# Copying the turned attention probabilities for two heads in one operation instead of one head by each of two engines

## What is computed

```python
p = softmax(q @ k.T * scale + bias)     # each query against a window of its grid neighbours
o = p @ v                               # 8 heads of 64 columns
mix = head_rms_norm(concat[o, gmlp, fourier])
x = x + mix @ w_out
```

## Time and profile before

| | |
|---|---|
| median of 3 runs | 2064.92 us (2064.7 to 2065.62) |
| span of the profiled execution, first to last instruction | 2062.8 us |
| own time of the profiled execution | not given apart from its span; the span is 2.1 us below the median |
| PE busy | 2042.2 us, 99% |
| DVE busy | 1419.9 us, 69% |
| ACT busy | 825.1 us, 40% |
| POOL busy | 227.8 us, 11% |

### The profile page before, as it was taken

One profiled execution on the slowest core, in us unless ns is written; L12 is line 12 of the kernel. 1 busy time (PEld: TensorE's weight loads), 2 busy tenths in 40 slices (PEclk: granted clock), 3 DMA queues, 4 the chain that ended last, 5 costly groups with the idle time before them and its releaser, 6 DMA issues.

```text
span 2062.8 us, 27797 instructions
## 1 busy us (share of the span) xinstructions
PE 2042.2 (99%) x10316; PEld 1698.2 (82%) x10316; DVE 1419.9 (69%) x2320; ACT 825.1 (40%) x1466; POOL 227.8 (11%) x135
## 2 busy tenths in 40 slices
PE   8999999999999999999999999999999999999998
PEld 7888788888888888888898887888888888888887
DVE  6323773789877778787833338647988777778877
ACT  4221683452333333444612227634433333344443
POOL 1332034200000000000023301441000000000000
PEclk9999999999999999999999999999999999999999
DMA  5222443224333236633221314441243323383333
GB/s 183 72 92 62 144 134 123 72 77 169 130 111 107 98 112 255 195 97 97 76 86 62 102 41 144 144 153 48 85 172 129 114 93 111 109 310 114 97 98 123
DMA packets 111060, 244.40 MB, mean 118 GB/s; under 512 B 13648, under 2 KB 18640, under 8 KB 110672
## 3 DMA queue, kind: packets, MB, share of 16 engines
q1 hardware_dynamic: 97056, 214.32, 32.4%
q10 hardware_dynamic: 13872, 28.31, 3.7%
HBM read 191.73 MB, written 50.86 MB: 118 GB/s over the span
## 4 chain that ended last, share of the span: by engine, by line
PE 92%; DVE 5%; issue 1%; ACT 1%; DMA 0%; ACTq 0%; POOL 0%; DVEq 0%
PE bank L1872 28%; PE bank L1874 28%; PE bank L1873 28%; PE bank L2036 2%; PE bank L2055 2%; PE bank L2020 2%; DVE s_lo L1233 1%; DVE t_lo L1536 0%; PE bank L1966 0%; PE bank L2077 0%; PE bank L1995 0%; PE bank L2070 0%; ACT logits L950 0%; DVE hid_cu L1649 0%; ACT s_hi L797 0%
## 5 line engine op out<-in xcount | busy, mean ns | idle before, releaser
L1872 PE MATMUL bank<-t_hi,s_hi 128*128 128x512 f32 (+1 forms) x1336 | 516.9, 387 | 0.8 <-DVE hid_cu L1649 0.5
L1873 PE MATMUL bank<-t_lo,s_hi 128*128 128x512 f32 (+1 forms) x1336 | 516.3, 386 | 0.0
L1874 PE MATMUL bank<-t_hi,s_lo 128*128 128x512 f32 (+1 forms) x1336 | 516.3, 386 | 0.0
L1872 PEld LDWEIGHTS bank<-t_hi,s_hi 128*128 128x128 f32 x1336 | 250.9, 188 | 52.6 <-DVE hid_cu L1649 1.4
L1874 PEld LDWEIGHTS bank<-t_hi,s_lo 128*128 128x128 f32 x1336 | 250.9, 188 | 50.9
L1873 PEld LDWEIGHTS bank<-t_lo,s_hi 128*128 128x128 f32 x1336 | 250.9, 188 | 50.6
L675 POOL TENSOR_TENSOR w_lo<-w_raw,w_hi 128x1024 fp32r<-128x1024 f32 x65 | 161.1, 2492 | 928.9 <-ACT w_hi L761 787.4
L1872 PE MATMUL bank<-b_hi,s_hi 128*128 128x512 f32 x528 | 206.0, 390 | 0.2
L1874 PE MATMUL bank<-b_hi,s_lo 128*128 128x512 f32 x528 | 205.5, 389 | 0.0
L1873 PE MATMUL bank<-b_lo,s_hi 128*128 128x512 f32 x528 | 205.4, 389 | 0.0
L1872 PE MATMUL bank<-h_hi,w_hi 128*128 128x512 f32 x512 | 201.1, 393 | 0.0
(11 more groups left out here) (218 smaller groups left out, 3187.2 us busy)
## 6 DMA issues: line engine op xcount, KB each, us to landing
w_g<-in_wg SPq DMA_DIRECT2D x44, 512.0 KB, 3.5
w_u<-in_wu SPq DMA_DIRECT2D x44, 512.0 KB, 4.4
t_raw<-hidden_t SPq DMA_DIRECT2D x88, 256.0 KB, 2.6
bias<-in_bias SPq DMA_DIRECT2D x24, 768.0 KB, 5.8
w_raw<-in_win SPq DMA_DIRECT2D x34, 512.0 KB, 3.8
t_raw<-hidden_b SPq DMA_DIRECT2D x66, 256.0 KB, 2.6
hidden_b<-hid_g SPq DMA_DIRECT2D x60, 256.0 KB, 2.0
hidden_t<-hid_x SPq DMA_DIRECT2D x44, 256.0 KB, 2.0
```

The lines of the kernel that those rows point to most:

```text
L1872: nc.tensor.matmul(bank, lh, rh, start=start, stop=False)
L1873: nc.tensor.matmul(bank, lh, rl, start=False, stop=False)
L1874: return nc.tensor.matmul(bank, ll, rh, start=False, stop=stop)
```

## The change

Banks 2 and 3 become one tensor of two banks, `TURNED`. One operation now copies both heads of a pair, 128 x 768 elements, out of it: DVE does so for even pairs, ACT for odd pairs. Each copy waits for both heads of its pair to be turned. PE turns a pair only when the copy of the whole pair before it is done, and `values(i)` waits for one engine's counter instead of two. The DVE copies of heads 4m-2 and the ACT copies of heads 4m+1 vanish from the program; the others stay at their places and become pair copies. PE's instructions stay the same and in the same order.

```diff
-        B = [ctx.enter_context(nc.psum_tensor(f"bank{i}", [P, HALF], F32)) for i in range(8)]
+        B = [ctx.enter_context(nc.psum_tensor(f"bank{i}", [P, HALF], F32)) for i in range(2)]
+        TURNED = ctx.enter_context(nc.psum_tensor("turned", [P, 2, HALF], F32))
+        B += [TURNED[:, 0, :], TURNED[:, 1, :]]
+        B += [ctx.enter_context(nc.psum_tensor(f"bank{i}", [P, HALF], F32)) for i in range(4, 8)]
...
-                def turned_odd(t):
-                    act.wait_ge(pt_full, l * 64 + t + 1)
-                    if t >= 4:
-                        act.wait_ge(pv_done, l * 64 + t - 3)
-                    nc.scalar.activation(PT[:, t % 4, :], B[3][:, 0:NKEY], ACT.Copy).then_inc(pt_act, 1)
+                def turned_odd(i):
+                    act.wait_ge(pt_full, l * 64 + 2 * i + 2)
+                    if i >= 2:
+                        act.wait_ge(pv_done, l * 64 + 2 * i - 2)
+                    nc.scalar.activation(PT[:, 2:4, :], TURNED[:, :, 0:NKEY], ACT.Copy).then_inc(pt_act, 1)
...
                 for i in range(SINGLE):
                     if i:
                         probs(2 * i)
-                        turned_odd(2 * i - 1)
+                        if i % 2 == 0:
+                            turned_odd(i - 1)
                         probs(2 * i + 1)
...
                     probs(4 * m)
-                    turned_odd(4 * m - 1)
+                    turned_odd(2 * m - 1)
                     probs(4 * m + 1)
...
-                    turned_odd(4 * m + 1)
                 tile_raw(5)
-                turned_odd(63)
+                turned_odd(31)
...
-                def turned_even(t):
-                    dve.wait_ge(pt_full, l * 64 + t + 1)
-                    if t >= 4:
-                        dve.wait_ge(pv_done, l * 64 + t - 3)
-                    nc.vector.tensor_copy(PT[:, t % 4, :], B[2][:, 0:NKEY]).then_inc(pt_dve, 1)
+                def turned_even(i):
+                    dve.wait_ge(pt_full, l * 64 + 2 * i + 2)
+                    if i >= 2:
+                        dve.wait_ge(pv_done, l * 64 + 2 * i - 2)
+                    nc.vector.tensor_copy(PT[:, 0:2, :], TURNED[:, :, 0:NKEY]).then_inc(pt_dve, 1)
...
-                    if i:
-                        turned_even(2 * i - 2)
+                    if i % 2:
+                        turned_even(i - 1)
...
                     logits(4 * m)
                     logits(4 * m + 1)
-                    turned_even(4 * m - 2)
                     if m % 2:
                         head_norms((m - 5) // 2)
                     logits(4 * m + 2)
                     logits(4 * m + 3)
                     if m % 2 == 0:
                         head_sums((m - 4) // 2)
-                    turned_even(4 * m)
-                turned_even(62)
+                    turned_even(2 * m)
...
                     if t < 2:
                         pe.wait_ge(k_raw, l * 8 + 3 + t)
-                    else:
-                        pe.wait_ge(pt_act if t % 2 else pt_dve, l * 32 + t // 2)
+                    elif t % 2 == 0:
+                        pe.wait_ge(pt_dve if t % 4 else pt_act, l * 16 + (t + 2) // 4)
...
-                    pe.wait_ge(pt_dve, l * 32 + i + 1)
-                    pe.wait_ge(pt_act, l * 32 + i + 1)
+                    pe.wait_ge(pt_act if i % 2 else pt_dve, l * 16 + i // 2 + 1)
...
-                        pe.wait_ge(pt_act if b == 3 else pt_dve, l * 32 + 32)
+                        pe.wait_ge(pt_act, l * 16 + 16)
```

## The result

The changed kernel is slower: 2076.14 us against 2065.14 us in medians of four runs each, +11.0 us; the ratio is 1.0052 with a 95% interval of 1.0036 to 1.0068. One of the four runs of the changed kernel took 3445.01 us at a granted clock of 0.557 (one later run of the kernel before took 2932.92 us at 0.654) and is in that median but not in the ratio; the other three took 2075.21, 2075.70 and 2076.58 us. The prediction was 2077 us in a range of 2070 to 2082.

The account below looks back on a forecast made before the run. PE was taken to bound the kernel. Per layer 1.0 + 0.55 + 5 x 0.87 + 0.3 = 6.2 us, 12.4 for both, took the span from 2062.8 to 2075.2; with the median 2.1 above, 2077 us, range 2070 to 2082.

Parts of the forecast that it names:

- What bounds it: Whole kernel: PE is busy 2042.2 of 2062.8 us, and its delays reach the end nearly microsecond for microsecond.
- Cost of the operations: Pair copies of 768 columns: 0.95 us on DVE, 0.80 on ACT, extrapolated from 384 and 512 columns.
- Rival 2: Nothing amortised: pair copies take 1.11 and 0.95 us, 18.6 us in all, 2083.5 us; chance 0.06.
- The odd m: m = 5 to 15, counted from T, the start of turn_pair: PE waits 0.87 us at values(2m-1).
- the signal: From the end of ACT's pair copy to the start of PE's values: 0.13 us.
- The split between DVE's queue and ACT's length: Odd m: 0.57 us from DVE's pair copy ahead of heads_copy and logits, 0.32 us from the longer ACT copy.
- The even m: m = 6 to 14, five per layer: no cost and no slack, ACT's copy covered by the four transposes of turn_heads.
- The single regime: Attention before m = 4: scores(3) slips 0.40 us, values(1) comes 0.71 late, later blocks add more, together 1.0 us.
- blocks 4 to 6: Single regime: late exponentials and ACT pair copies add 0.02, 0.20 and 0.10 us.
- m = 4 and m = 15: Per layer: 0.55 us at values(7) in m = 4; only about 0.3 us in m = 15, which waits already.
- the first rival: Only the longer copy counts, DVE's queue absorbs its 0.40 us: 4.8 us in all, 2069.7 us; chance 0.12.
- The third: Engines freed: DVE and ACT gain 0.1 us per m, waits of 1.5 us per layer go, 2062 us; chance 0.03.

Follow-up runs that it names:

- the run with even pairs only: Changed kernel's DVE pair copies for even pairs only, odd pairs copied one head by each engine as in the kernel before: 2072.28 us, ratio 1.0032.
- the run with odd pairs alone: ACT pair copies for odd pairs only, even pairs copied one head by each engine as in the kernel before: 2068.84 us, ratio 1.0017.
- the run with the piece rounded last: ACT pair copies for even pairs only, odd pairs as before, and in m = 15 a weight piece rounded behind the last exponentials: 2073.93 us, ratio 1.0043.
- the run before it: Against the kernel before, ACT copies even pairs in one operation at each m's end, odd pairs one head by each engine: 2066.15 us, ratio 1.0004.

## Why the prediction was right, step by step

- **What bounds it.** PE's waits went to the end in full: 5.4 us per layer, twice, in a span 11.1 us longer. No later stretch gave any back.
- **Cost of the operations.** 958 and 789 ns, taken as 0.95 and 0.80. The extrapolation from 384 and 512 columns holds to 768 across two PSUM banks for ACT (0.80) and is 0.03 us short for DVE (0.93, which I had raised to 0.95 without a reason). Rival 2 (nothing amortised, 1.11 and 0.95) is out.
- **The odd m.** 0.78 us, predicted 0.87. Every event up to the end of ACT's copy came within 0.02 us of its computed place. The term that was mis-sized is the last: I gave the signal from ACT to PE 0.13 us, and in the changed kernel the matmul starts 0.05 us behind the copy's end (286.29 + 0.79 to 287.13). In the run with even pairs only it took 0.14, as in the kernel before. The twelve traces show what goes with it: wherever PE waited for a copy, it started 0.04 to 0.06 us behind the copy's end if the copy's counter is the first or the only one that the code waits for there, and 0.14 to 0.15 if a wait for another counter stands ahead of it. The change took one such wait out of `values`; with the 0.09 us of it the sum would be 0.87, as predicted. No run varied this alone.
- **The split between DVE's queue and ACT's length.** Predicted 0.57 and 0.32 less a slack of 0.02, measured by halves 0.55 and 0.23: DVE's side is its 0.57 less the slack, ACT's its 0.32 less the 0.09 of the shorter signal.
- **The even m.** No cost, as predicted: the distance over an even m stayed at 5.21 to 5.22, with ACT's pair copy under the cover of `turn_heads`.
- **The single regime.** 0.77 us, predicted 1.0. Scores(3) slipped 0.40 us as computed, and up to turn(2) the cost is 0.63 (3.27 + 4.05 against 3.65 + 3.04) where 0.71 stood, again the signal. Of the 0.32 us given to blocks 4 to 6, 0.15 came, all in the step from turn(3) to turn(4).
- **m = 4 and m = 15.** 0.53 and 0.17, predicted 0.55 and 0.3. The chain of m = 4 came out at 0.61 and I rounded it down for "other work"; what took the 0.09 off is again the signal, so the 0.55 is a lucky figure.
- **Two slips in the working.** PE waited 0.6 us per layer for ACT's copy before the change, 0.59 of it in m = 15, so it isn't true that the copies cost no PE time. And the range of 2070 to 2082 does not take in the first rival's 2069.7.
- **The total.** 6.2 us per layer was 0.8 too much: about 0.6 by the signal (0.4 in five odd m, the rest in m = 15, m = 4 and values(1)), and 0.2 in blocks 4 to 6.
- **The rivals.** The first (only the longer copy, 2069.7 us) would have had PE wait 0.3 us in odd m; it is what the run with odd pairs alone shows, 2068.84, and what is missing there is DVE's side. The third (engines freed) fails in the changed kernel itself: each wide operation is shorter than two narrow ones (958 ns against twice 556), and logits(4m) still come at T + 2.39. The run that frees DVE of 32 copies is no faster than before either, though new waits of 0.46 us per layer stand against any gain in it.
- **The rule.** The Trainium skill, page Perfetto Trace Analysis, section Optimizing Scalar/DVE Operations, says that where engines aren't saturated but cause bubbles elsewhere, breaking instructions up can let work complete sooner. The runs agree, with small numbers: cutting DVE's pair copy in two brought the values 0.09 us forward in each odd m, though it added operations.

## What to carry to other kernels

Grouping operations saves their fixed part on their own engine (here some 0.1 us of each pair) and costs latency: the group waits for its last input, holds up everything queued behind it, and delivers its first output with its last. Where another engine is the bound, count the second and not the first: write down, from one anchor on the bounding engine, when each link of the chain starts, and compare the last with the time at which it was due. If a group is wanted all the same, put it on the engine and at the place whose next customer comes latest; and when an operation is moved later, follow its result through every engine that it passes, not only to the wait that one wants to remove.

## What the runs showed of the hardware

PE's granted clock halved behind a single gap: in the run with the piece rounded last, PE stood 2.6 us, and the granted clock went from 1.00 to 0.50 (2.4 to 1.2 GHz; the 0.58 of the window above is a mean of both levels). From 313 us on it was 1.00 again. At 0.50, matmuls of 512 columns began 0.42 to 0.45 us apart in place of 0.23, and a turn took 1.48 us in place of 0.87. The second layer repeats it with the fall a little later: PE stood 2.61 us, the clock was still 1.00 from 1332.70 to 1333.40, and 0.50 from 1333.54 to 1336.50. What it cost is read between two points that lie outside the slow stretch, turn(30) and the last values:

```profile
303.93 0.87 PE L2047 MATMUL turned<-ident,logits 128*128 128x128 f32 x6
...
314.94 1.53 PE L2067 MATMUL bank<-probs_t,v_band 128*64 128x128 f32 x24
```

These are 11.01 us against 6.51 in the run before it (304.85 to 311.36), in both layers: 4.5 us, of which PE stood 2.6. By turn(31), in the middle of the slow stretch, only 3.4 of them are seen (6.61 against 3.23). The gaps of the changed kernel left the clock at 1.00: one of 0.97 us at 233.00 (1.00 from 226 to 252), and one near 0.7 us every 10 us behind it:

```profile
252.00:300.00 48.00, 44.64 (x474) 36.39 (x474) 35.97 (x97) 35.04 (x95) 12.32 (x16) 1.00 0.44 126
```

A price per microsecond of waiting taken from these short gaps is therefore too low for the long one.
